# Attention of a two-layer mixer kernel: three PSUM banks for turned tiles, four for scores

## The chip, the cores and the metric

The program runs on one core of one Trainium2 chip. The metric is the device time in microseconds. Four engines do the work: TensorE (PE: matrix products and transpositions, writing to the eight banks of PSUM), VectorE (DVE), ScalarE (ACT) and GpSimd (POOL); SyncE (SP) issues the transfers. Each engine works through its own instructions in order and waits on semaphores for the others.

## What is computed

Two layers, each with three branches that read one normalised input: grouped Fourier mixing, multi-scale pooling and latent attention. The attention is what the change touches:

```python
def one(qblk):
    s = jnp.einsum('bqhd,bkhd->bhqk', qblk, k, preferred_element_type=jnp.float32) * scale
    p = jax.nn.softmax(s, axis=-1).astype(v.dtype)
    return jnp.einsum('bhqk,bkhd->bqhd', p, v)
```

There are 8 heads, 1024 sample tokens with 1280 keys laid out (each sample tile sees 1152 of them) and 128 prompt tokens that see 128 keys.

## The kernel before

**Tiles and steps.** A head has nine tiles of 128 queries: eight of the sample, whose scores come in three pieces of 128x384 (`parts` is 3), and one of the prompt with one piece of 128x128. With 8 heads that makes `TILES` = 72 tiles and `STEPS` = 75 steps in each layer. In this text a head's step j is the step s with s = 9h + j, and a piece is numbered 0, 1, 2.

**Products in three passes.** Scores and projections are products of a high and a low part of each operand (`three_pass`, lines 1607 to 1609), so one piece of scores is three matmuls.

**What a step does.** In step s TensorE goes through `PE_STEP`: it turns (transposes) a piece of the probabilities of tile s - 1 (`turn`, line 1798; with the last piece also the inverse of the row sums, line 1802), makes a piece of the scores of tile s + 1 (`scores`), and multiplies turned tiles of an earlier pair with the values (`mix`, lines 1823 and 1824); this three times. Six of a head's nine steps end with a product beside them that makes the queries or the keys of the next head (`beside_pe`). VectorE takes the largest score of each piece (line 1450), the negative maximum of the row (1456), the low part of each turned piece (`turned_low`, 1463), the row sum and its inverse (1469, 1474), the low part of keys (1420) and the scaled queries (1416), and adds the halves of a mixed group (`unmix`, 1484). ScalarE goes, in step s, through: the lift of a mixed group (867, in some steps), the high part of turned piece 0 of tile s - 1 (`turned_high`, 848), the exponentials of piece 0 of tile s (`exps`, 832, an ACTIVATE and the read of its sum behind it), and the same for pieces 1 and 2.

**Banks.** `bank_plan` gives each kind of work (a phase) a first bank and a number of banks; item n of a phase goes to bank first + n mod banks. TensorE, before it writes item n (`pe_takes`), waits until the bank's previous item was read: a score piece is released by its exponentials, a turned piece by `turned_low`, queries and keys by VectorE's line 1416 or 1420, a mixed group by `unmix`. Turned pieces, queries and keys share one phase, `attn`, in the order of `attention_items`: the pieces of a tile, then what lies beside. Before the change `score` has the five banks 0 to 4, `mixed` bank 5 and `attn` banks 6 and 7. So a turned piece waits for the item two before it, and a score piece for the exponentials of the piece five before it. For step s this is: piece 0 of tile s + 1 waits for exponentials 1 of tile s - 1, piece 1 for exponentials 2 of tile s - 1, piece 2 for exponentials 0 of tile s.

**Around it.** The last head has nothing beside it, and in two of its steps (`GATE_STEPS`) ScalarE splits a weight tile of the next stage (line 693) behind its exponentials.

Of the kernel before, what the change touches and what calls it, by code (L numbers as in the profile page):

```python
# [30 lines left out]
TT = TOK // P  # L31
# [4 lines left out]
HEADS = 8  # L36
# [71 lines left out]
def bank_plan():  # L108

    phases = []  # L110
    def add(layer, name, first, banks, count):
        phases.append(((layer, name), first, banks, count))
    add(0, "vec", 6, 1, 1)
    add(0, "mod", 0, 6, 16)
    add(0, "modt", 6, 1, 1)
    add(0, "norm", 6, 2, NCH * KF)
    for l in range(DEPTH):
        add(l, "tok", 0, 3, 2 * TT)
        add(l, "feat", 0, 6, 3 * len(FEAT_COLS))
        add(l, "turn", 0, 6, 14)  # L120
        add(l, "pool", 6, 2, 6)
        add(l, "val", 6, 2, KS)
        add(l, "seq", 6, 2, 12)
        add(l, "chan", 0, 6, 6)
        add(l, "attn", 6, 2, len(attention_items()))
        add(l, "score", 0, 5, HEADS * (3 * TT - 2))
        add(l, "mixed", 5, 1, HEADS * GROUPS)
        add(l, "gate", 0, 3, 3 * 3 * KF)
        add(l, "branch", 3, 3, 3 * 3 * KF)
        if l == 0:  # L130
            add(l, "later", 6, 2, later(GATE_ROWS)[0])
        add(l, "gbc", 6, 2, 4)
        if l == 0:
            add(l, "last", 6, 2, len(LATER) - later(GATE_ROWS)[0])
        add(l, "out", 0, 6, 3 * TT)
        if l + 1 < DEPTH:
            add(l + 1, "norm", 6, 2, NCH * KF)
    used = [0] * 8
    plan = {}
    for key, first, banks, count in phases:  # L140
        plan[key] = (first, banks, [used[first + i] for i in range(banks)])
        for i in range(banks):
            used[first + i] += len(range(i, count, banks))
    return plan
# [19 lines left out]
def later(u):  # L164

    units = 3 * KF - 2
    return range(len(LATER) * min(u, units) // units, len(LATER) * min(u + 1, units) // units)
# [9 lines left out]
GROUPS = 5  # L177
# [3 lines left out]
def parts(m):  # L181

    return 1 if m % TT == 8 else 3
# [62 lines left out]
def beside(s):  # L246

    h, j = divmod(s, TT)
    if j in BESIDE_STEPS and h + 1 < HEADS:
        n = BESIDE_STEPS.index(j)  # L250
        return [("qk"[n // 3], h + 1, n % 3)]
    return []


def attention_items():

    order = [(kind, 0, i) for kind in "kq" for i in range(3)]
    for s in range(STEPS):
        if 1 <= s <= TILES:
            order += [("t", s - 1, g) for g in range(parts(s - 1))]  # L260
        order += beside(s)
    return {key: n for n, key in enumerate(order)}


def hybrid_step(nc, x_prompt, x_sample, cache_ckv, cache_krope, c, c_ctx, norm_g, w_mod, b_mod, w_in,
                pool_w, pool_scale, q_norm_g, w_q_up, kv_norm_g, w_kv_up, w_br_a, w_br_b, w_br_c,
                w_out, final_norm_g, tab, y_prompt, y_sample, new_ckv, new_krope, park_hi, park_lo, rows_mid):
    plan = bank_plan()


# [1683 lines left out]
```

## Time and profile before

| | |
|---|---|
| median of 3 runs | 2224.97 us (2221.03 to 2226.98) |
| the profiled execution | 2222.64 us, span 2220.4 us |
| PE busy | 2131.5 us, 96% of the span |
| DVE, ACT, POOL busy | 1090.4, 886.7, 653.6 us (49%, 40%, 29%) |
| chain that ended last | PE 84%, DVE 7%, ACT 4%, issue 3% |
| granted TensorE clock over the span | 0.993 |

Busy time of PE is modelled from the starts of matmuls, so a busy PE need not be at its peak. A row of the timeline has the start, the duration, the engine with its line and operation, output and inputs, and in brackets the idle time of the engine before it with what released it. `PE L1607 ... kT,qT` is the first of the three matmuls of a score piece; `ACT L832 ACTIVATION_READ_ACCUMULATOR` ends a piece's exponentials.

### The profile page before, as it was taken

How to read it: one execution, taken by the hardware profiler on the slowest of the kernel's cores; microseconds unless marked ns; L12 is line 12 of the kernel's file. 1: busy time of each engine (PE TensorE's matmuls, PEld its weight loads, DVE VectorE, ACT ScalarE, POOL GpSimd, SP SyncE). 2: the span in 40 equal slices, each digit the busy share in tenths (PEclk: the TensorE clock that was granted, in tenths of full speed). 3: DMA queues.
4: the chain of work that ended last, by engine and by line, in shares of the span. 5: the costliest groups of instructions: out<-in, count | busy, mean ns of one | idle time of the engine just before them, and what ended most of it. 6: DMA issues, size and time to landing. Idle time of an engine off the chain costs nothing.

```text
span 2220.4 us, 35875 instructions
## 1 busy us (share of the span) xinstructions
PE 2131.5 (96%) x13185; PEld 2035.3 (92%) x13185; DVE 1090.4 (49%) x2823; ACT 886.7 (40%) x2223; POOL 653.6 (29%) x560
## 2 busy tenths in 40 slices
PE   7999999999999999999999999999999999999997
PEld 5899878888899999999989997888888999999997
DVE  2441268888864667663162314888886111120213
ACT  2521267777831212113152214777777112111312
POOL 1323122322322234333441311222323223343342
PEclk8999999999999999999999999999999999999999
DMA  9811000000343333224255100000005111111232
GB/s 275 267 33 31 26 1 1 1 1 1 121 155 85 95 83 100 78 63 143 74 197 163 40 1 26 1 2 1 1 14 192 48 36 48 40 46 39 65 124 85
DMA packets 194622, 155.67 MB, mean 70 GB/s; under 512 B 8637, under 2 KB 186001, under 8 KB 193425
## 3 DMA queue, kind: packets, MB, share of 16 engines
q1 hardware_dynamic: 194448, 153.38, 22.2%
q8 instruction: 106, 1.74, 0.3%
q14 instruction: 68, 0.55, 0.1%
HBM read 124.89 MB, written 28.48 MB: 69 GB/s over the span
## 4 chain that ended last, share of the span: by engine, by line
PE 84%; DVE 7%; ACT 4%; issue 3%; DMA 1%; POOL 0%; SPq 0%; DVEq 0%; POOLq 0%; ACTq 0%
PE ps L1607 23%; PE ps L1609 23%; PE ps L1608 23%; PE ps L1798 5%; PE ps L1823 3%; PE ps L1824 2%; DVE partmax L1450 1%; DVE probsT L1463 1%; PE ps L1617 1%; DVE kT L1420 1%; ACT kT L879 1%; PE ps L1841 1%; ACT probsT L848 1%; DVE xn_high L1201 1%; ACT probs L832 1%
## 5 line engine op out<-in xcount | busy, mean ns | idle before, releaser
L1607 PE MATMUL ps<-xn_high,split_br 128*128 128x384 f32 x1584 | 531.8, 336 | 0.0
L1609 PE MATMUL ps<-xn_high,split_br 128*128 128x384 f32 x1584 | 529.5, 334 | 0.0
L1608 PE MATMUL ps<-xn_low,split_br 128*128 128x384 f32 x1584 | 529.3, 334 | 0.0
L960 ACT ACTIVATE sigmoids<-ps 128x384 f32<-128x384 f32 x144 | 70.4, 492 | 613.5 <-PE ps L1609 613.5
L1608 PEld LDWEIGHTS ps<-xn_low,split_br 128*128 128x128 f32 x1584 | 297.5, 188 | 0.0
L1607 PEld LDWEIGHTS ps<-xn_high,split_br 128*128 128x128 f32 x1584 | 297.4, 188 | 0.0
L1609 PEld LDWEIGHTS ps<-xn_high,split_br 128*128 128x128 f32 x1584 | 297.3, 188 | 0.0
L1002 POOL TENSOR_TENSOR split_br<-raw,split_br 128x1024 fp32r<-128x1024 f32 x82 | 198.2, 2418 | 320.4 <-ACT split_br L693 320.4
L1463 DVE TENSOR_TENSOR probsT<-ps,probsT 128x384 fp32r<-128x384 f32 x384 | 213.1, 555 | 70.1 <-ACT sum_inv_rows L855 42.7
L832 ACT ACTIVATE probs<-ps,negmax 128x384 f32<-128x384 f32 (+1 forms) x400 | 229.1, 573 | 29.3 <-DVE negmax L1456 28.7
L1798 PE MATMUL ps<-ident,probs 128*128 128x128 f32 x1168 | 197.5, 276 | 31.0 <-DVE kT L1420 15.8
L848 ACT ACTIVATE probsT<-ps 128x384 fp32r<-128x384 f32 x384 | 188.6, 491 | 79.9 <-PE ps L1798 46.7
L1450 DVE TENSOR_REDUCE partmax<-ps 128x1 f32<-128x384 f32 (+1 forms) x400 | 212.1, 534 | 2.0 <-PE ps L1609 1.8
L1541 DVE TENSOR_TENSOR products<-ps,sigmoids 128x384 f32<-128x384 f32 x96 | 53.5, 557 | 293.0 <-PE ps L1609 240.3
L1798 PEld LDWEIGHTS ps<-ident,probs 128*128 128x128 f32 x1168 | 132.0, 140 | 70.6 <-issue 65.3
L1136 POOL TENSOR_TENSOR merged<-merged,products 128x384 f32<-128x384 f32 x90 | 92.2, 1025 | 334.7 <-DVE products L1541 333.8
L1607 PE MATMUL ps<-split_br,xn_high 128*128 128x256 f32 (+1 forms) x576 | 182.2, 316 | 5.3 <-DVE xn_low L1204 5.0
L1609 PE MATMUL ps<-split_br,xn_low 128*128 128x256 f32 (+1 forms) x576 | 178.7, 310 | 0.0
L1608 PE MATMUL ps<-split_br,xn_high 128*128 128x256 f32 (+1 forms) x576 | 178.7, 310 | 0.0
L1823 PE MATMUL ps<-probsT,head_values 128*128 128x256 f32 x576 | 156.3, 291 | 12.0 <-DVE mixed_out L1484 12.0
L1607 PE MATMUL ps<-kT,qT 128*128 128x384 f32 (+1 forms) x400 | 163.3, 408 | 1.6 <-ACT probs L832 1.0
L1091 POOL TENSOR_TENSOR branch<-mixed_out,branch 64x256 f32<-64x256 f32 (+1 forms) x80 | 54.2, 678 | 335.3 <-DVE mixed_out L1484 334.4
(227 smaller groups left out, 4197.4 us busy)
## 6 DMA issues: line engine op xcount, KB each, us to landing
raw<-in_w_in SPq DMA_DIRECT2D x74, 512.0 KB, 3.9
raw<-in_w_mod SPq DMA_DIRECT2D x48, 512.0 KB, 5.0
park_high<-xn_high SPq DMA_DIRECT2D x6, 1536.0 KB, 6.4
park_low<-xn_low SPq DMA_DIRECT2D x6, 1536.0 KB, 10.6
xn_high<-park_high SPq DMA_DIRECT2D x2, 4608.0 KB, 16.0
rows<-in_x_sample SPq DMA_DIRECT2D x16, 512.0 KB, 6.8
raw<-in_w_out SPq DMA_DIRECT2D x16, 512.0 KB, 6.5
rows_mid<-rows SPq DMA_DIRECT2D x9, 512.0 KB, 2.6
```

The source lines that it names most:

```text
L832: a.activation((P0, P1)[m % 2][:, c * CH:c * CH + w], PS[:, b, 0:w], ACT.Exp, bias=negmax[:, m % 2:m % 2 + 1], accum_out=partsum[:, m % 2, ...
L848: ins = a.activation(turned_place(m, gg, 0), PS[:, b, 0:n * P].rearrange("p (k c) -> p k c", k=n), ACT.Copy)
L960: a.activation(sig[:, ch, :], PS[:, b, 0:CH], ACT.Sigmoid).then_inc(bank_free[b], 1)
L1002: g.tensor_tensor(d[:, 1], raw_unit(n), d[:, 0].bitcast(F32), ALU.subtract).then_inc(S("split_low"), 1)
L1136: g.tensor_tensor(Y[:, u % KF, sl], Y[:, u % KF, sl], prod[:, q % 2, :], ALU.add).then_inc(S("y_sum"), 1)
L1450: v.tensor_reduce(partmax[:, m % 2, c:c + 1], PS[:, b, 0:w], AX.X, ALU.max).then_inc(S("partmax"), 1)
L1463: v.tensor_tensor(turned_place(m, gg, 1), PS[:, b, 0:n * P].rearrange("p (k c) -> p k c", k=n), turned_place(m, gg, 0).bitcast(F32), ALU.s ...
L1607: mm(out, wh, xh, start=first, stop=False)
L1608: mm(out, wh, xl, start=False, stop=False)
L1609: return mm(out, wl, xh, start=False, stop=last)
L1798: ins = nc.tensor.transpose(PS[:, b, q * P:(q + 1) * P], (P0, P1)[m % 2][:, (3 * gg + q) * P:(3 * gg + q + 1) * P], ident[:])
L1823: mm(PS[:, b, 0:w], vhl, xh, start=(kt == 0 or gr == 4), stop=False)
```

## The change

Within the attention stage of each layer, `attn` gets banks 5, 6 and 7 instead of 6 and 7, `score` banks 0 to 3 instead of 0 to 4, and `mixed` moves from bank 5 to bank 4. The Fourier products `chan`, which run shortly before, get five banks instead of six. No instruction is added, removed or reordered; only banks and the counts in the waits change.

```diff
-        add(l, "chan", 0, 6, 6)
-        add(l, "attn", 6, 2, len(attention_items()))
-        add(l, "score", 0, 5, HEADS * (3 * TT - 2))
-        add(l, "mixed", 5, 1, HEADS * GROUPS)
+        add(l, "chan", 0, 5, 6)
+        add(l, "attn", 5, 3, len(attention_items()))
+        add(l, "score", 0, 4, HEADS * (3 * TT - 2))
+        add(l, "mixed", 4, 1, HEADS * GROUPS)
```

## Rows read from the trace of the kernel before

**Rows 1.** Busy time by stretch: stretch, length, engines, PEclk, DMA share, GB/s

```profile
40.00:60.00 20.00, 12.10 (x82) 9.23 (x81) 14.25 (x26) 10.73 (x18) 9.03 (x6) 0.68 0.95 316
...
508.00:549.00 41.00, 38.20 (x264) 34.88 (x264) 34.33 (x99) 31.79 (x98) 10.25 (x14) 1.00 0.00 1
```

**Rows 2.** Waits of PE, whole span: us in total, times, longest us

```profile
PE ps L1798 <- DVE kT L1420: 15.8, 42, 0.5
PE ps L1798 <- DVE probsT L1463: 12.5, 34, 0.7
PE ps L1823 <- DVE mixed_out L1484: 12.0, 20, 0.7
```

**Rows 3.** Timeline, start of the attention, where a score waits for exponentials

```profile
306.34 0.19 ACT L832 ACTIVATION_READ_ACCUMULATOR probs<-ps,negmax 128x1 f32 x1
...
306.59 0.45 PE L1607 MATMUL ps<-kT,qT 128*128 128x384 f32 x1 [0.50 <-ACT probs L832]
```

**Rows 4.** Timeline, head 5, step 4, with nothing waited for on PE

```profile
523.95 0.49 PE L1798 MATMUL ps<-ident,probs 128*128 128x128 f32 x3
...
524.48 0.49 ACT L848 ACTIVATE probsT<-ps 128x384 fp32r<-128x384 f32 x1 [1.39 <-PE ps L1798]
...
524.86 0.57 ACT L832 ACTIVATE probs<-ps,negmax 128x384 f32<-128x384 f32 x1
...
525.29 0.42 PE L1607 MATMUL ps<-kT,qT 128*128 128x384 f32 x1
...
525.33 0.20 ACT L832 ACTIVATION_READ_ACCUMULATOR probs<-ps,negmax 128x1 f32 x1
```

**Rows 5.** Timeline, head 5, step 2: score pieces 1 and 2, exponentials 0 and 1

```profile
515.71 0.42 PE L1607 MATMUL ps<-kT,qT 128*128 128x384 f32 x1
...
515.83 0.20 ACT L832 ACTIVATION_READ_ACCUMULATOR probs<-ps,negmax 128x1 f32 x1
...
516.88 0.42 PE L1607 MATMUL ps<-kT,qT 128*128 128x384 f32 x1
...
517.17 0.22 ACT L832 ACTIVATION_READ_ACCUMULATOR probs<-ps,negmax 128x1 f32 x1
```

**Rows 6.** Timeline, head 5, step 5: a turned piece that waits, score piece 1, exponentials 0

```profile
529.99 0.52 PE L1798 MATMUL ps<-ident,probs 128*128 128x128 f32 x3 [0.47 <-DVE kT L1420]
...
530.26 0.42 PE L1607 MATMUL ps<-kT,qT 128*128 128x384 f32 x1
...
530.33 0.20 ACT L832 ACTIVATION_READ_ACCUMULATOR probs<-ps,negmax 128x1 f32 x1
```

**Rows 7.** Timeline, head 5, step 6: exponentials 0 and score piece 1

```profile
535.24 0.20 ACT L832 ACTIVATION_READ_ACCUMULATOR probs<-ps,negmax 128x1 f32 x1
...
535.71 0.42 PE L1607 MATMUL ps<-kT,qT 128*128 128x384 f32 x1
```

**Rows 8.** Timeline, head 5, step 7: inverse of the row sums and its turning

```profile
540.89 0.16 DVE L1474 RECIPROCAL sum_inv<-rowsum 128x1 f32<-128x1 f32 x1
...
541.29 0.27 PE L1802 MATMUL ps<-ident,sum_inv 128*128 128x128 f32 x1
```

**Rows 9.** Timeline, step 0 of head 5: score piece 1, the mix behind it, exponentials 0

```profile
506.45 0.33 PE L1607 MATMUL ps<-kT,qT 128*128 128x384 f32 x1
...
507.73 0.39 PE L1823 MATMUL ps<-probsT,head_values 128*128 128x256 f32 x1 [0.60 <-DVE mixed_out L1484]
...
507.85 0.19 ACT L832 ACTIVATION_READ_ACCUMULATOR probs<-ps,negmax 128x1 f32 x1
```

**Rows 10.** Timeline, last head (7), steps 2 and 5: score piece 1, exponentials 0

```profile
595.29 0.42 PE L1607 MATMUL ps<-kT,qT 128*128 128x384 f32 x1
...
596.04 0.20 ACT L832 ACTIVATION_READ_ACCUMULATOR probs<-ps,negmax 128x1 f32 x1
...
607.45 0.42 PE L1607 MATMUL ps<-kT,qT 128*128 128x384 f32 x1
...
609.14 0.20 ACT L832 ACTIVATION_READ_ACCUMULATOR probs<-ps,negmax 128x1 f32 x1
```

## The prediction

> **What bounds the kernel now.** I began with the busy times by stretch. TensorE is the bound everywhere; in the attention one head lasts some 41 us, of which TensorE is busy 38.2 us, VectorE 34.3 and ScalarE 31.8 [rows 1]. So TensorE loses a few microseconds a head there, and the two other engines have little room. Next came TensorE's waits [rows 2]. Three of them lie in the attention: a turned piece waits 42 times for the low part of the keys (15.8 us) and 34 times for the low part of an earlier turned piece (12.5 us), both of them waits for one of the two `attn` banks, and a mixed group waits 20 times for its only bank (12.0 us). The change gives a bank to the first two kinds, 28.3 us in all, and takes one from the scores, which in this list do not appear with more than a start-up wait. The question is therefore how close to the limit the scores' five banks already are. For that I read single steps on the timeline, and put beside each score piece the end of the exponentials that will have to release it.
>
> **The rule of the new wait.** With five banks, score piece 1 of tile s + 1 waits for the exponentials of piece 2 of tile s - 1, which are long done. With four it waits for piece 0 of tile s, and piece 2 for piece 1 of tile s. Where such a wait shows now, at the first tile, TensorE starts at 306.59, 0.06 us after the exponentials end at 306.34 + 0.19 [rows 3]; I take 0.06 us as the latency.
>
> **An ordinary step.** In step 4 of head 5 TensorE turns piece 0 at 523.95 and reaches score piece 1 at 525.29, 1.34 us later. ScalarE meanwhile was idle for 1.39 us, takes the turned piece as soon as it is there (524.48), then the exponentials of piece 0 (524.86), which end at 525.33 + 0.20 = 525.53 [rows 4]. The score piece could then start at 525.59: 0.30 us late. Since ScalarE here waits for TensorE itself, its chain begins with TensorE's own step, so the 0.30 us come back in each such step and are not swallowed by an earlier delay. Steps 1 and 3 have the same form and give about 0.30 and 0.26.
>
> **The other steps of a head.** In step 2 ScalarE also makes the high part of the queries between exponentials 0 and 1. Piece 1 (515.71, released at 516.03 + 0.06) is 0.38 late, piece 2 (516.88, released at 517.39 + 0.06) 0.57 [rows 5]. The second contains the first, because both exponentials depend on turnings that come earlier in the step: 0.57.
> Step 5 has one of the waits that the third bank removes, 0.47 us before turned piece 1. But score piece 1 behind it starts at 530.26 and would be released at 530.53 + 0.06 [rows 6]: it is late by 0.33 even against a start that already contains the 0.47. The wait only moves, from the turned piece to the score, and grows.
> In step 6 the same 0.47 stands before the turned piece, and the exponentials end at 535.44, before the score's 535.71 [rows 7]. Here 535.71 - 535.50 = 0.21 us are won, not more.
> In steps 7 and 8 two or three waits for an `attn` bank go, and no score piece meets a late release. What is late next is the inverse of the row sums: it is ready at 541.05 and turned at 541.29 [rows 8], and VectorE gets to it through an unbroken queue (low parts, maxima, the weights of a later head). So of these waits only 0.24 - 0.06 = 0.18 us come out.
> Step 0 is the costly one. Nothing but two score pieces and one mix lies there. Score piece 1 starts at 506.45 and would wait until 507.85 + 0.19 + 0.06 = 508.10, 1.65 us. The mix behind it now waits 0.60 us for its own bank [rows 9]; that wait is swallowed, and 1.05 us remain. In other heads the mix waits up to 0.7 us [rows 2], and the wait is counted only from the modelled end of a matmul, while matmuls overlap; I take 0.92.
>
> **The sum.** A head: 0.92 + 0.30 + 0.57 + 0.26 + 0.30 + 0.33 - 0.21 - 0.18 = 2.29 us; in heads that also split new values ScalarE is a little further behind in step 2, and I take 2.35. Seven heads in each of two layers: 14 x 2.35 = 32.9 us.
> The last head has no work beside it, so its steps are short for ScalarE and the releases later. In step 2 score piece 1 starts at 595.29 and is released at 596.24 + 0.06: 1.01 us, some 0.1 of which replaces a wait further on. In step 5, behind a weight split, it starts at 607.45 and is released at 609.34 + 0.06, 1.95 us [rows 10]; the mix behind it now waits up to 0.7 us [rows 2], which go, leaving about 1.2. Step 3, also behind a split, has the same form. With two steps of the ordinary form, one more at about 0.35 and the 0.92 of step 0: 0.92 + 0.3 + 0.9 + 1.2 + 0.35 + 1.2 + 0.35 = 5.2 us, twice 10.4.
> Together 32.9 + 10.4 = 43.3 us. The profiled execution took 2222.6 us, so it would be 2265.9; the median of the runs shown lies 2.3 us higher, so I predict 2268 us, 1.9% slower.
> The edit of `chan` costs nothing: its sixth item then takes the bank of its first, which VectorE has read by then. The first keys of a layer take bank 5, which VectorE is still reading, where now the third keys wait for a bank; one wait takes the place of the other. No queue of transfers is moved: SyncE waits for the same items, later by what the attention loses, and the transfers before the next stage have that much more time.
>
> **Bounds.** The terms that no row shows as a wait are the distances between a score and its future release. From below: if half of the distances vanish because ScalarE gets its turned pieces earlier through the third bank, some 20 us remain, 2245. From above: if the lateness of piece 2 adds to that of piece 1 instead of containing it, each head loses another 1 to 1.5 us, 16 to 24 us more, 2290.
>
> **Rivals.**
> Faster: the third bank pays what it shows. The mechanism is the wait of turned pieces for an `attn` bank; its price is 15.8 + 12.5 = 28.3 us [rows 2], so 2225 - 28 = 2197. It decides where exponentials 0 end before the score piece comes up, as in step 6 [rows 7]. Against it stand steps 1 to 5 and 0, where they end later [rows 4 to 6, 9]. Chance 0.05.
> Nearly the same: the turned pieces, coming earlier, let ScalarE run ahead in all steps but step 0. Then 16 x 0.92 = 14.7 us are lost there and 16 x (0.21 + 0.18) = 6.2 won, 2233; with a few more of the bank waits won it is within the noise. Against it: ScalarE in step 4 waits for turned piece 0, which waits for no bank now [rows 4]. Chance 0.08, half of it within 0.3%, which is about what a measurement of this kernel can tell from no change.
> Much slower: delays compound, as under the upper bound, or a mix, a row sum or queries of the next head become late too, 2300. VectorE is 84% busy in the attention [rows 1] and could be what does it. Chance 0.09.
> The clock: it is granted in full throughout the attention, with TensorE busy 93% of the time; at 40 to 60 us, with TensorE busy 12.1 of 20 us, it was 0.68 [rows 1], that is, partly at the lower level of 1.2 GHz. The change leaves some 88% busy and no idle time over 2 us. If the lower level came in one head of each layer, its 38 us of matmuls would double, 2268 + 76 = 2344. Chance 0.02.
> The Trainium skill has a rule against this change, in "TensorE: Matmul & The Clock Gate", section "A second HAM failure mode: psum-queue depth-cycling": a kernel that cycles through PSUM banks can idle shortly between groups so often that the clock swings between its levels. By that rule the last rival would be the result; the trace of before has such short waits some 76 times in this stage and shows no swing, so it does not bear the rule out here.
>
> **How the numbers follow.** The main case has 0.76: 2268, own range 2250 to 2285. For 8 in 10 I take in both bounds: 2243 to 2290. Slower by over 0.3%: 0.76 + 0.04 + 0.09 + 0.02 = 0.91; within: 0.04; faster: 0.05.
>
> **What would show it right or wrong.** Right: TensorE's list of waits has a new line, scores (line 1607) waiting for exponentials (line 832), with some 60 to 80 waits a layer, two kinds of them (piece 1 in steps 0 to 6, piece 2 in step 2), the longest about 1.7 us and one such a head; the waits of turned pieces for line 1420 are gone and those for line 1463 nearly; the mix at a head's beginning waits for `unmix` in few places; a head lasts 43 us. Wrong: score waits only at the heads' beginnings; or a head of about 40 us; or the granted clock under 1 in the attention.

## The result, and the profile after

The changed kernel takes 2261.71 us (median of 4 runs, 2260.11 to 2264.41) against 2223.46 us (2221.03 to 2226.98) for the kernel before on the same chip: 1.7% slower, ratio 1.0174 with a 95% interval of 1.016 to 1.0187. The forecast was 2268. The profiled execution took 2262.91 us, span 2260.7; its span is 40.3 us longer than that of the profiled execution before.

The waits of TensorE, whole span (us in total, times, longest us), to be held against [rows 2]:

```profile
PE ps L1607 <- ACT probs L832: 60.6, 88, 1.6
PE ps L1634 <- ACT xn_value L726: 11.4, 12, 2.1
PE ps L1823 <- DVE mixed_out L1484: 8.9, 16, 0.8
...
PE ps L1802 <- DVE sum_inv L1474: 3.8, 14, 0.3
```

The two kinds of wait for an `attn` bank are gone, 28.3 us in all, and a new line stands on top: 88 score pieces wait for exponentials, 60.6 us. The mix still waits for its bank, 8.9 us for 12.0, but elsewhere: mostly at the beginning of a head before (7 of 10 in a layer), in step 7 of each head now (8 in a layer). The waits of the attention add up to 15.8 + 12.5 + 12.0 + 1.0 = 41.3 us before (the 1.0 is two score waits at the two starts) and to 60.6 + 8.9 + 3.8 = 73.3 after: +32.0. Another +7.6 us is TensorE's busy time. Only a small part of it is longer matmuls: the first matmul of a score piece takes 0.44 to 0.45 us behind a wait instead of 0.42, some 2 us for 88 waits, and the turned pieces get a little shorter. The rest is overlap. The records of matmuls that follow each other overlap and are counted once, and the first matmul behind a wait overlaps with none, so a wait costs more than the list says:

```profile
PE 2139.1 (95%) x13185; PEld 2045.5 (90%) x13185; DVE 1090.8 (48%) x2823; ACT 886.3 (39%) x2223; POOL 653.2 (29%) x560
...
PE 80%; ACT 8%; DVE 5%; issue 5%; DMA 1%; POOL 0%; SPq 0%; ACTq 0%; DVEq 0%; POOLq 0%
```

These are the busy times and the chain that ended last, from the page of after: ScalarE's share of the chain doubled from 4% to 8%, at the cost of TensorE's. The work is the same (the other engines' busy times are within 0.5 us of before; PE's was 2131.5).

From score piece 1 in step 0 of head 5 to the same piece of head 6 it is now 42.66 us (518.64 to 561.30); it was 40.46 (506.45 to 546.91). Busy time by stretch of after (columns as in [rows 1]), the attention of layer 0 and a stretch about as long as a head:

```profile
305.00:651.00 346.00, 308.44 (x2076) 282.15 (x2076) 265.62 (x756) 253.13 (x762) 92.31 (x110) 1.00 0.09 32
523.20:566.00 42.80, 38.43 (x261) 35.12 (x260) 34.25 (x99) 31.29 (x97) 9.07 (x12) 1.00 0.00 1
```

TensorE is busy 38.4 of these 42.8 us, at full clock, where it was 38.2 of 41.0 [rows 1]. From head 5 to head 6, between the two score pieces named, its busy time grew by 0.5 us and its idle time by 1.7. From the first score to the last mix the attention went from 329.1 to 347.9 us in layer 0 and from 329.6 to 349.9 in layer 1: 39.1 of the 40.3 us. The other 1.2 lie outside it, 0.3 ahead of the first score and 0.9 between the two attentions, where TensorE's waits are those of before but the clock falls once for a short stretch (at 1184 us), which it does not in the execution before.

Two steps of head 5, timeline of after. First step 4, answering [rows 4]:

```profile
536.37 0.49 PE L1798 MATMUL ps<-ident,probs 128*128 128x128 f32 x3
...
536.89 0.49 ACT L848 ACTIVATE probsT<-ps 128x384 fp32r<-128x384 f32 x1 [1.40 <-PE ps L1798]
...
537.28 0.57 ACT L832 ACTIVATE probs<-ps,negmax 128x384 f32<-128x384 f32 x1
...
537.74 0.20 ACT L832 ACTIVATION_READ_ACCUMULATOR probs<-ps,negmax 128x1 f32 x1
538.00 0.19 PEld L1607 LDWEIGHTS ps<-kT,qT 128*128 128x128 f32 x1 [0.29 <-ACT probs L832]
538.00 0.44 PE L1607 MATMUL ps<-kT,qT 128*128 128x384 f32 x1
```

From turned piece 0 to score piece 1 it is now 1.63 us instead of 1.34, and the score starts 0.06 us after the exponentials end (537.74 + 0.20). ScalarE's chain hangs on the turned piece exactly as before: 0.52 us to the high part, 0.39 to the exponentials.

Then step 0, answering [rows 9]:

```profile
518.40 0.19 ACT L832 ACTIVATION_READ_ACCUMULATOR probs<-ps,negmax 128x1 f32 x1
...
518.64 0.45 PE L1607 MATMUL ps<-kT,qT 128*128 128x384 f32 x1 [1.59 <-ACT probs L832]
...
519.28 0.28 PE L1823 MATMUL ps<-probsT,head_values 128*128 128x256 f32 x1
```

The score waits 1.59 us; the mix behind it, which waited 0.60 before [rows 9], no longer does.

### The profile page after: what moved, and what is told of

Same layout as the page of the kernel before. It is cut to its first block, busy times and chain, and to the rows that moved or that the text cites. A ratio compares the mean times of both kernels' runs of the same rounds, so it can differ in the third digit from the quotient of the medians.

```text
span 2260.7 us, 35875 instructions
## 1 busy us (share of the span) xinstructions
PE 2139.1 (95%) x13185; PEld 2045.5 (90%) x13185; DVE 1090.8 (48%) x2823; ACT 886.3 (39%) x2223; POOL 653.2 (29%) x560
## 4 chain that ended last, share of the span: by engine, by line
PE 80%; ACT 8%; DVE 5%; issue 5%; DMA 1%; POOL 0%; SPq 0%; ACTq 0%; DVEq 0%; POOLq 0%
PE ps L1607 24%; PE ps L1609 22%; PE ps L1608 22%; ACT probs L832 3%; PE ps L1798 3%; PE ps L1823 2%; PE ps L1824 2%; ACT probsT L848 2%; DVE partmax L1450 1%; DVE probsT L1463 1%; PE ps L1841 1%; DMA raw<-in_w_mod 1%; PE ps L1802 1%; PE ps L1617 1%; ACT mixed_out L867 1%
## 5 line engine op out<-in xcount | busy, mean ns | idle before, releaser
L1607 PE MATMUL ps<-kT,qT 128*128 128x384 f32 (+1 forms) x400 | 168.0, 420 | 63.1 <-ACT probs L832 60.6
L1607 PEld LDWEIGHTS ps<-kT,qT 128*128 128x128 f32 x400 | 76.0, 190 | 97.6 <-ACT probs L832 92.7
```

What stands on the lines that cost most here:

```text
L1607: mm(out, wh, xh, start=first, stop=False)
```

## The experiments

All ran beside the kernel before, whose median was 2222.2 us (experiments 1 to 4), 2221.5 (5, 6 and 8) and 2222.9 (7, 9 and 10).

**The theory**: all of the loss comes from the scores, which with four banks wait for a release one piece nearer than with five, and the third `attn` bank gives back only what steps 6 to 8 show. **Its rivals**: a side effect of the placement (which bank number, `mixed`, `chan`), delays that compound, or a loss that the third bank causes.

### 1. One part alone: four score banks, `attn` left at two

```diff
-        add(l, "score", 0, 5, HEADS * (3 * TT - 2))
+        add(l, "score", 0, 4, HEADS * (3 * TT - 2))
```

> Four banks for scores as in the changed kernel, but turned pieces, queries and keys stay at two banks (bank 4 stays empty, chan at six banks). Theory (the loss is the scores' wait for the exponentials; the third attn bank is worth only 0.7 us a head, since what is late behind it is a release by ScalarE or the inverse of the row sums): 2273 us, 11 us over the changed kernel, with line 1607 waiting for line 832 by about 60 us in all and the waits for lines 1420 and 1463 back in part. Rival 1 (the third bank pays what the waits of before show, 28 us, and the scores lose correspondingly more): 2290. Rival 2 (what slows the changed kernel is the move of chan, mixed or attn to other banks, not the scores' fourth bank): 2224, as before.

Measured 2265.93 us (2264.57 to 2267.88), ratio 1.0196 (1.0181 to 1.0211). TensorE's waits of this kernel:

```profile
PE ps L1607 <- ACT probs L832: 36.0, 40, 1.5
PE ps L1798 <- DVE kT L1420: 15.9, 42, 0.5
...
PE ps L1798 <- DVE probsT L1463: 11.5, 28, 0.7
```

So the loss is there without the third `attn` bank, and without any phase in another place: here no bank number changes but that the scores lose bank 4. The third bank is worth 4.2 us by the medians. The waits that it removes are still here, 27.4 us, and removing them, as the change does, gains a sixth of that. Head by head, this kernel is 2.4 to 2.6 us longer than before and the changed one 2.0 to 2.3, so the bank gives about 0.3 us a head: 0.4 in steps 6 to 8, of which step 0 takes back 0.1. The expectation had put it at 0.7 us a head, with a median of 2273, and the score waits at 60 us; they are 36.0, since in steps 5 and partly 2 and 3 the turned pieces wait here in place of the scores behind them. The timeline of this kernel in step 5 of head 5 shows how such a wait misleads:

```profile
542.86 0.52 PE L1798 MATMUL ps<-ident,probs 128*128 128x128 f32 x3 [0.47 <-DVE kT L1420]
543.46 0.44 PE L1607 MATMUL ps<-kT,qT 128*128 128x384 f32 x1
```

The score starts 0.60 us after the turned piece, where it was 0.27 at [rows 6]: it is 0.33 us late behind a wait of 0.47. In the changed kernel the turned piece doesn't wait and the score waits 0.98. The time at which the score can start is the same, measured from the step ahead:

```profile
543.34 0.45 PE L1607 MATMUL ps<-kT,qT 128*128 128x384 f32 x1 [0.98 <-ACT probs L832]
```

(The changed kernel.) From score piece 1 of step 4 to score piece 1 of step 5 it is 5.33 us here, 5.34 in the changed kernel and 4.97 before.

### 2. The bank given to the mix instead

```diff
-        add(l, "score", 0, 5, HEADS * (3 * TT - 2))
-        add(l, "mixed", 5, 1, HEADS * GROUPS)
+        add(l, "score", 0, 4, HEADS * (3 * TT - 2))
+        add(l, "mixed", 4, 2, HEADS * GROUPS)
```

> Four banks for scores, two for mixed groups (4 and 5), two for attn: the bank taken from the scores goes to the mixed groups. Theory: the waits for the single mixed bank are hidden by the scores' wait at a head's beginning, 8.9 us of them are left in the changed kernel and most of those lie where a later wait catches them; so 2268 to 2272, 2 to 4 us under the run with the empty bank. Rival (the mixed bank is what the attention lacks, 12 us of wait before): 2260.

Measured 2264.75 us (2263.99 to 2269.56), ratio 1.0197 (1.018 to 1.0214). The mix's 12.0 us of waits vanish from the list and the score's stay at 36.0 us in 40 waits; the time is that of experiment 1 within its noise, and 3 us under what was expected. The mix's wait at a head's beginning had been swallowed by the score's, as the prediction said of step 0. Nor does the place of `mixed` matter: it has bank 4 and 5 here instead of 5, and the time is the same.

### 3. One bank further: three for scores, four for `attn`

```diff
-        add(l, "chan", 0, 6, 6)
-        add(l, "attn", 6, 2, len(attention_items()))
-        add(l, "score", 0, 5, HEADS * (3 * TT - 2))
-        add(l, "mixed", 5, 1, HEADS * GROUPS)
+        add(l, "chan", 0, 4, 6)
+        add(l, "attn", 4, 4, len(attention_items()))
+        add(l, "score", 0, 3, HEADS * (3 * TT - 2))
+        add(l, "mixed", 3, 1, HEADS * GROUPS)
```

> One bank more taken from the scores: three for scores, four for attn, one for mixed groups. Each score piece then waits for the exponentials of the same piece of the tile before. Theory: in an ordinary step piece 0 comes 0.25 us after the turning of piece 0 and would be released 1.65 us after it, 1.4 us late; the turning of the next piece stands behind it and begins the next chain of 1.65 us, so pieces 1 and 2 are late by 1.2 to 1.6 us too. Some 4 us in each of 128 full tiles, in place of the 0.3: 2262 + 128 x 3.8 = 2750 us, 2550 to 2800. Rival (the loss grows by as much as for the first bank taken, 38 us): 2300.

Measured 2824.45 us in a single execution, 602 us more than before and just above the expected 2550 to 2800. Its list of waits, and below it the busy time by stretch in the attention of layer 0, for the whole stage and for 40 us of it:

```profile
PE ps L1607 <- ACT probs L832: 432.5, 334, 2.1
```

```profile
305.00:905.00 600.00, 389.58 (x1924) 334.51 (x1925) 273.43 (x723) 246.11 (x726) 86.30 (x103) 0.81 0.03 12
460.00:500.00 40.00, 27.74 (x114) 23.87 (x114) 15.40 (x36) 14.27 (x41) 9.16 (x10) 0.66 0.00 1
```

Now 334 of the 400 score pieces wait, each for the exponentials of the same piece of the tile before. The waits of the attention are 395 us more than before (432.5 and 3.5 for the inverse of the row sums, for 41.3), and TensorE's busy time is 212 us more (2343.5 for 2131.5). The second part goes with the clock: granted at 0.81 over the stage and 0.66 in the second stretch, that is, partly at the lower level of 1.2 GHz. In the stage shown TensorE is busy 390 us for 1924 matmuls, against 308 for 2076 in the changed kernel.

### 4. The changed kernel with the mix ahead of score piece 1 in step 0

```diff
-                for what, c in PE_STEP:
+                order = list(PE_STEP)
+                if s % TT == 0 and s:
+                    order[4], order[5] = order[5], order[4]
+                for what, c in order:
```

> The changed kernel, but in a head's step 0 TensorE does the mix before score piece 1 instead of behind it. Theory: the mix waits for its bank until where it did before the change, and the score behind it then finds its bank nearly free; step 0 costs 0.65 us in place of 0.9: 2262 - 16 x 0.25 = 2258 us, and the longest wait of line 1607 for line 832 falls from 1.6 to under 1 us. Rival (the wait for the exponentials at step 0 is not on the path): 2262, unchanged.

Measured 2255.58 us (2255.17 to 2256.25), ratio 1.0149 (1.0134 to 1.0164): 6.1 us less than the changed kernel, where 4 were expected. Held beside the changed kernel's trace, whose span is 7.7 us longer, step 0 is 0.2 to 0.4 us shorter in each of 14 heads, 4.5 us in all; another 1.6 us is a short stretch at the lower clock that the changed kernel has in its last head and this one has not. The waits:

```profile
PE ps L1607 <- ACT probs L832: 38.6, 74, 1.2
PE ps L1823 <- DVE mixed_out L1484: 26.6, 30, 1.4
```

The score's fall by 22.0 us and the mix's rise by 17.7. Step 0 can be eased only by a part, since both of its pieces wait for work that VectorE finishes at about the same time (experiment 9 shows this again).

### 5. The changed kernel with exponentials 0 ahead of turned piece 0 on ScalarE

If the chain turned piece, high part, exponentials is what delays score piece 1 in steps 1, 3, 4 and 5, then exponentials that run first release the bank earlier.

```diff
                 for c in range(3):
+                    if c == 0 and s < TILES:
+                        exps(s, 0)
...
-                    if s < TILES and c < parts(s):
+                    if c and s < TILES and c < parts(s):
                         exps(s, c)
```

> The changed kernel, but ScalarE makes the exponentials of piece 0 of tile s before the high part of turned piece 0 of tile s - 1, instead of behind it. The bank of piece 0 is then free some 0.4 us earlier in each step. Theory (the loss in steps 1 to 5 is that release, which hangs behind the turned piece on ScalarE): piece 1 is no longer late in steps 1, 3, 4 and 5, piece 2 in step 2 still is; 1.2 us a head come back, 2262 - 19 = 2243 us, and the waits of line 1607 for line 832 fall from 60.6 to about 40 us. Rival (what holds the step up is the pair turned piece and its low part on VectorE, which now come 0.7 us later): 2262 or more.

Measured 2260.51 us (2260.31 to 2260.68), ratio 1.0175 (1.0158 to 1.0192): no gain. The waits of TensorE (line numbers here are two higher than in the changed kernel):

```profile
PE ps L1609 <- ACT probs L832: 42.6, 52, 1.6
PE ps L1804 <- DVE sum_inv L1476: 22.3, 28, 1.4
```

The mechanism is right, 36 of the 88 score waits are gone and 18.0 us with them. But a new wait takes their place: 22.3 us for the inverse of the row sums, which was 3.8. VectorE works in a fixed order and makes the low part of turned piece 0 before the row sum and the maximum; with the high part later, all of its queue moves back.

### 6. The same edit in the kernel before

> The same order on ScalarE in the kernel before (five banks for scores, two for attn). Theory: no score piece waited there, so nothing is to be won; the low part of turned piece 0 and with it its bank come later, and with two banks piece 2 of the same step may wait for it: 2222 to 2235 us. Rival (the order is worth something by itself, whatever the banks): 2205.

Measured 2255.24 us (2255.04 to 2255.94), ratio 1.0152 (1.0137 to 1.0168): 33.7 us slower than before, which neither side had expected. TensorE's waits:

```profile
PE ps L1800 <- DVE probsT L1465: 45.3, 68, 1.5
PE ps L1800 <- DVE kT L1422: 15.8, 42, 0.5
```

With two `attn` banks the later low part also holds the bank of a turned piece: 45.3 us instead of 12.5. With three, in experiment 5, that wait does not occur. So with this order a third bank has much to do, and with the order before it has the 4.2 us of experiment 1.

### 7. Experiment 5 with VectorE's queue mended

```diff
-DVE_STEP = (("beside", 0), ("unmix", 0), ("low", 0), ("sum", 0), ("max", 0), ("low", 1),
+DVE_STEP = (("beside", 0), ("unmix", 0), ("sum", 0), ("max", 0), ("low", 0), ("low", 1),
```

> The changed kernel with the exponentials of piece 0 first on ScalarE and with VectorE's row sum and maximum before the low part of turned piece 0; the mix stays behind the score in step 0. The run without VectorE's part won 18 us of score waits and lost 22 us to a new wait for the inverse of the row sums, which stands on VectorE behind the later low part. Theory: with VectorE's order that wait goes and the 1.2 us a head show: 2262 - 16 x 1.2 = 2243 us, 6 us over the run that also has the mix first. Rival (another wait of VectorE's takes its place): 2255 or more.

Measured 2241.65 us (2240.2 to 2243.05), ratio 1.0082 (1.0068 to 1.0097): 20.1 us less than the changed kernel, as expected. The wait for the inverse is gone from the list, so experiment 5 had failed for the reason given. With four score banks and three for `attn`, a gain of half of the loss can be had by the order in which ScalarE and VectorE take their work: against the changed kernel steps 1, 3 to 6 and 8 are each 0.2 to 0.5 us shorter, and step 0 is 0.8 us longer, more where the clock falls. What VectorE's order would be worth in the kernel before was not tried. TensorE's waits and the busy time by stretch in the attention of each layer:

```profile
PE ps L1609 <- ACT probs L832: 56.5, 66, 2.4
```

```profile
305.00:645.00 340.00, 307.31 (x2085) 287.99 (x2086) 268.21 (x755) 252.94 (x764) 91.81 (x111) 0.98 0.09 33
1400.00:1740.00 340.00, 307.22 (x2099) 287.45 (x2100) 270.11 (x755) 255.26 (x767) 92.59 (x111) 0.99 0.09 35
```

The score waits add up to hardly less than after (56.5), yet the time is 20 us less: the waits of the ordinary steps fell and those of step 0 grew from 1.6 to 2.4 us. A list of waits counts what is waited for at one place, not what the place delays.

### 8. The two together: experiments 4 and 7

> The changed kernel with the exponentials of piece 0 first on ScalarE, the mix before score piece 1 in step 0 on TensorE, and on VectorE the row sum and the maximum of piece 0 before the low part of turned piece 0, so that VectorE does not stand behind the later turned piece. Theory: the gains add, 2243 - 6 = 2237 us, and VectorE's order gives 0 to 5 more: 2235. Rival (the first two share one gain): 2243.

Measured 2241.17 us (2233.14 to 2247.51), ratio 1.0087 (1.0059 to 1.0114). By the medians the mix ahead of the score adds nothing to experiment 7 (0.5 us); by the fastest run of each it adds 7.1. Its runs lie 14 us apart, and the granted clock over the span goes with them: 0.995 at 2233.14 us, 0.993 at 2237.16, 0.987 at 2245.19 and 0.986 at 2247.51. Where neither profile has a stretch at the lower clock, a head with the mix ahead is 0.2 to 0.4 us shorter than in experiment 7, as in experiment 4. So the gain of experiment 4 is there, and the clock hides it in the medians; what lowers the clock in some executions and not in others stays open. The expected 2235 us is met by the fastest runs alone. A further kernel was this one with the exponentials first in all three pieces:

```diff
-                    if c == 0 and s < TILES:
-                        exps(s, 0)
+                    if s < TILES and c < parts(s):
+                        exps(s, c)
                     if turned(s - 1, c) is not None:
                         turned_high(s - 1, turned(s - 1, c))
-                    if c and s < TILES and c < parts(s):
-                        exps(s, c)
```

> As the run with all three reorderings, but ScalarE makes the exponentials of each piece before the high part of the turned piece of the same number. Theory: piece 2 in step 2 (0.57 us late) is then released in time too, 0.5 us a head: 2235 - 8 = 2227. If with that no score piece waits outside step 0, the third attn bank can pay what the kernel before shows, up to 28 us, and the time falls under 2222: the best case is 2205. Rival (turned pieces late, the inverse of the row sums and the mix behind them become the bound): 2240 or more.

Measured 2246.99 us (2243.3 to 2250.99), ratio 1.0115 (1.01 to 1.013): not the 2227 hoped for. Score piece 1 waits for exponentials 0 alone in the ordinary steps, and these already ran first. The wait for the inverse of the row sums is back in part (3.4 us), and the clock is 0.98 to 0.99 in both layers.

### 9. The kernel before with `unmix` ahead of the last maxima in step 0

At a head's beginning the mix waits for `unmix`, which VectorE does behind the maxima of the step before. This puts it ahead of the last of them.

```diff
+                early = s % TT == 0 and s and mixed_in(s - 1)
+                if early:
+                    unmix(*mixed_in(s - 1))
...
+                    if what == "unmix" and early:
+                        continue
```

> The kernel before (five banks for scores), but at a head's step 0 VectorE adds the halves of the mixed group before it takes the last maximum and the negative maximum of the tile, instead of behind them. Theory (in step 0 of the five-bank kernel the bound is the mixed group's bank, released by that addition, and the exponentials of the step have slack): the mix starts some 0.4 us earlier in each of 16 heads, 12.0 us of wait fall to about 6, and the time falls by 6 to 7 us to 2215. Rival (the exponentials, now 0.4 us later, are as close as the mix): 2222, unchanged.

Measured 2223.12 us (2222.65 to 2224.15), ratio 1.0001 (0.9992 to 1.001), where 2215 was expected. The mix's waits fall from 12.0 to 3.1 us, and nothing is gained. The timeline at step 0 says why (line 1612 is the score's 1607 here):

```profile
507.93 0.19 ACT L832 ACTIVATION_READ_ACCUMULATOR probs<-ps,negmax 128x1 f32 x1
...
508.17 0.19 PEld L1612 LDWEIGHTS ps<-kT,qT 128*128 128x128 f32 x1 [0.31 <-ACT probs L832]
508.18 0.44 PE L1612 MATMUL ps<-kT,qT 128*128 128x384 f32 x1
```

Score piece 2, with five banks too, starts 0.06 us after the exponentials of piece 0 of its step (508.12), so it takes over the place of the mix. In step 0 the mix and score piece 2 are about equally late. With four banks it is piece 1, ahead of the mix in TensorE's order, that waits for these same exponentials; that is why the bank costs so much there.

### 10. The same edit in the changed kernel

> The same edit in the changed kernel (four banks for scores). Theory: there step 0 is bound by the exponentials of piece 0, for which score piece 1 waits 1.6 us, and their negative maximum now comes 0.42 us later: 2262 + 16 x 0.42 = 2268 us, the same edit with the opposite sign. Rival (step 0 is bound by the mixed group in both kernels): 2255.

Measured 2281.7 us (2280.8 to 2283.57), ratio 1.0265 (1.0251 to 1.028): 20.0 us slower than the changed kernel, where 6 were expected. Waits and busy time by stretch, both layers:

```profile
PE ps L1612 <- ACT probs L832: 66.8, 88, 2.2
```

```profile
305.00:655.00 350.00, 309.66 (x2036) 283.68 (x2037) 264.39 (x752) 251.35 (x760) 89.94 (x107) 0.98 0.08 30
1413.00:1770.00 357.00, 315.87 (x2072) 289.22 (x2071) 267.10 (x758) 254.06 (x764) 92.98 (x110) 0.98 0.08 31
```

The 88 score waits grow by 6.2 us, as expected. The rest goes with the granted clock, 0.98 in both layers where the changed kernel has 1.00, and 0.987 over the span instead of 0.994. There are ten short stretches at the lower level in the attention, 34 us in all, where the changed kernel has one of 3.4 us. Each begins within about 1 us of the end of a step 0's score wait. A head whose step 0 has such a stretch is 1.8 to 2.2 us longer than in the changed kernel, one without 0.3 to 0.6: the expected 0.4 is right for the latter, and a stretch adds about 1.5.

## Why the prediction was right

**The rule of the new wait** holds to the number: 0.06 us from the end of the exponentials to the score in step 4, as at [rows 3]. So does the mechanism: experiment 1 has the loss with the scores' bank alone.

**The ordinary step.** Predicted 0.30 in step 4, measured 0.29 (1.63 against 1.34 us); step 3, predicted 0.26, gave 0.24; step 1, predicted 0.30, some 0.30. That each step pays anew is right: ScalarE waited 1.40 us for turned piece 0 and its queue began with it.

**Step 2** gave its 0.57, the second lateness containing the first. But the step that followed was overlooked: behind piece 2 stands the product of the next head's queries. Before, piece 2 began at 516.88 [rows 5] and the next turned piece 1.86 us later; after, 1.71, though the list of waits names nothing there. In the changed kernel:

```profile
529.19 0.45 PE L1607 MATMUL ps<-kT,qT 128*128 128x384 f32 x1
529.83 0.34 PE L1607 MATMUL ps<-qhatT,wq_head 128*128 128x384 f32 x1
530.37 0.34 PE L1607 MATMUL ps<-qhatT,wq_head 128*128 128x384 f32 x1
530.90 0.49 PE L1798 MATMUL ps<-ident,probs 128*128 128x128 f32 x3
```

Here 0.15 us are given back, and 0.40 in heads that split values. This is one term that makes the prediction too high, by about 0.15 us a head: I took heads that split values as slower (2.35 instead of 2.29), and they are not.

**Step 5** gave 0.35 for 0.33: the wait moved from the turned piece to the score, which now waits 0.98. In other words, one of the waits that the change removes, for VectorE, turned into a longer one for ScalarE.

**Steps 6 to 8** gave 0.20 (step 6) and 0.24 (7 and 8) for 0.21 and 0.18. Held beside experiment 1 they give about 0.4 us, and step 0 takes back 0.1. But what is late next in step 7 was not the inverse of the row sums, as the prediction had it. In step 7 of head 5 of the changed kernel:

```profile
550.05 0.42 PE L1607 MATMUL ps<-kT,qT 128*128 128x384 f32 x1
...
552.00 0.52 PE L1798 MATMUL ps<-ident,probs 128*128 128x128 f32 x3
553.16 0.38 PE L1823 MATMUL ps<-probsT,head_values 128*128 128x256 f32 x1 [0.65 <-DVE mixed_out L1484]
...
554.07 0.27 PE L1802 MATMUL ps<-ident,sum_inv 128*128 128x128 f32 x1
```

The turned pieces wait for nothing now, and the mix behind them waits 0.65 us for its only bank. From the score to the mix it is 3.11 us; before, with two waits of 0.38 and 0.19 ahead of the turned pieces, it was 3.10:

```profile
537.15 0.42 PE L1607 MATMUL ps<-kT,qT 128*128 128x384 f32 x1
...
538.89 0.52 PE L1798 MATMUL ps<-ident,probs 128*128 128x128 f32 x3 [0.38 <-DVE probsT L1463]
...
540.25 0.39 PE L1823 MATMUL ps<-probsT,head_values 128*128 128x256 f32 x1
```

(The kernel before.) The two bank waits became one for `unmix`, with no gain up to there; the inverse then comes 0.91 us behind the mix instead of 1.04, and those 0.13 us are the gain of step 7. In step 8 it is the inverse, as predicted: it is waited for 14 times, 3.8 us in all. The size was near, the reason was right for one of the two steps. A kernel with more banks for both was not tried: eight don't allow it beside four for scores.

**Step 0** gave 0.88 to 1.02 in heads 1 to 7 (1.00 in head 5) for 0.92, with a wait of 1.59 for the 1.65 worked out. The first head's gave 0.56 in each layer.

**The sum.** Counted from step 1 to the next head's step 1, the heads with work beside them grew by 2.0 to 2.3 us instead of 2.35 (the first, from its first score on and with both steps 0 in it, by 2.70). The last head, without its step 0, was put at 5.2 - 0.92 = 4.3 us and grew by 3.2 in layer 0: step 2 gave 0.43 for 0.9, step 5 0.89 for 1.2 and step 3 1.08 for 1.2. In layer 1 it grew by 4.7, about 1.5 of it from a stretch at the lower clock in step 3, 2.6 us there for the 1.1 of layer 0. In all +40.3 us for +43.3; the sum was made to 2265.9 for an execution that took 2262.9. Some of this nearness is luck: 1.5 us of the 40.3 are that stretch and 1.2 lie outside the attention, and no term of the sum stood for either. The terms themselves came to 37.6 us for 43.3.

**The number of waits**, 60 to 80 a layer, was too high: 44 a layer are listed. Steps 1 and 4 are hardly among them, though each costs 0.3 us: in step 4 the record of the turned pieces ahead ends only 0.05 us before the score starts, and so short an idle time is not listed. Piece 2 in step 2, the second kind of wait that was foretold, is not listed either. The listed sum, 60.6 us, is above the loss, since the bank waits that they replace went with them.

**The rivals.** *Faster* fell with the reason against it: the exponentials end late in steps 0 to 5. *Nearly the same* needed ScalarE to run ahead; it waits for the turned piece as before. *Much slower* did not come: lateness in a step does not add up. In step 2 of head 5 score piece 1 lost 0.50 us against the turned piece ahead of it, and piece 2 only 0.19 more. *The clock* is 1.00 in both layers to two places, but not untouched: in the last head of layer 1 there is a stretch of 3.4 us at the lower level (the prediction's sign of being wrong, in small), which costs 1.5 us; the attention of the execution before has none. Experiments 3 and 10 show how the clock takes more.

## What to carry to other kernels

Before a bank (or buffer) is moved from one kind of work to another, read what the giving side has to spare: for each of its writes the distance to the release it would then wait for. No list of waits shows this, and here that distance was 0.3 us short in the ordinary steps and 1.6 us in one step of nine. Even afterwards the list shows only a part, since a wait that the overlapping records of matmuls cover is not in it. A wait in the list is worth its length only where the next item in the same queue is not itself held as long: of 28.3 us of bank waits some 4 were to be had.

## What the runs showed of the hardware

In the attention the granted clock falls, where it does, in short stretches beside waits of TensorE, and the length of the wait alone does not decide it. The kernel before has none of these stretches there. The changed kernel has one, in step 3 of the last head of layer 1, behind score waits of 0.45 and 1.21 us (at 1717.00 and 1719.33):

```profile
1717.00:1719.00 2.00, 1.11 (x6) 0.84 (x6) 1.14 (x5) 1.95 (x4) 0.28 (x1) 1.00 0.00 0
1719.00:1721.00 2.00, 1.68 (x8) 1.68 (x9) 1.97 (x6) 1.22 (x5) 1.69 (x2) 0.73 0.00 0
1721.00:1723.00 2.00, 2.00 (x10) 2.00 (x9) 0.34 (x2) 1.09 (x4) 1.57 (x2) 0.50 0.00 0
```

The same step of layer 0, with a wait of 1.20, has none. Experiment 1 has a stretch at the same place behind a wait of 1.19, experiment 2 none behind one of 1.21. None follows the changed kernel's fourteen waits of 1.5 to 1.6 us in steps 0. Experiments 4 to 6 also have no wait over 1.6 us in the attention and no stretch. Where the wait of step 0 is longer, stretches come, but not each time: beside 10 of 14 waits of 1.8 to 2.2 us in experiment 10 (0.98 in both layers), beside 4 of 12 of 2.4 us in experiment 7 (0.98 and 0.99), and beside 1 of 12 of 2.0 to 2.2 us in the profiled execution of experiment 8, whose layer 0 has 1.00:

```profile
305.00:640.00 335.00, 304.43 (x2094) 284.94 (x2095) 269.79 (x757) 254.36 (x766) 92.42 (x112) 1.00 0.10 35
```

In experiment 3, with 334 waits up to 2.1 us and TensorE busy 65% of the stage, the clock was 0.81. What was seen is that these go together; no run changed the length of a wait and nothing else.

The Trainium skill, "TensorE: Matmul & The Clock Gate", section "A second HAM failure mode: psum-queue depth-cycling", says that idling shortly between groups while cycling through PSUM banks can make the clock swing. Experiments 3 and 10 agree with it (0.81 and 0.98); the changed kernel, with 88 such waits, shows it once (1.00 to two places in both layers).
